# The end of each stage token tile by token tile: the last two output blocks finish the first tile early, and the second tile is normalised in halves on two engines

## The reference

```
f = swiglu(rms_norm(x, g0)) ;  x = x + 0.5 * rms_norm(f, g1)      # ffn0 -> "p0"
m = short_conv_mixer(rms_norm(x, g2)) ;  x = x + rms_norm(m, g3)  # conv -> "pc"
f = swiglu(rms_norm(x, g4)) ;  x = x + 0.5 * rms_norm(f, g5)      # ffn1 -> "p1"
k, v = rms_norm(x, g_kv) @ w_kv
...                                                               # ffn2 -> "p2", attention -> "pa", ffn3 -> "p3"
swiglu(h) = (silu(h @ w_gate) * (h @ w_up)) @ w_down              # 1024 -> 2816 -> 1024
```

## Time and profile before

| | |
|---|---|
| median of 3 runs | 2194.36 us (2194.2 to 2194.81) |
| the profiled execution's own time | 2194.22 us |
| its span in the profile | 2192.4 us |
| busy: PE / DVE / ACT / POOL | 88% / 59% / 35% / 19% |
| chain that ended last | PE 65%, DMA 15%, DVE 8%, POOL 4%, ACT 3% |
| mean granted TensorE clock | 0.927 |

### The profile page before, as it was taken

The page is one execution under the profiler, slowest core; times in us unless marked ns, Lnnn a source line. Parts: engine busy times, 40 slices in busy tenths (PEclk is TensorE's granted clock), DMA queues, the critical chain, the costliest instruction groups (busy, mean ns, idle before and its releaser), DMA issues.

```text
span 2192.4 us, 30637 instructions
## 1 busy us (share of the span) xinstructions
PE 1919.4 (88%) x11270; PEld 1548.3 (71%) x11270; DVE 1285.4 (59%) x2435; ACT 765.1 (35%) x1183; POOL 416.8 (19%) x536
## 2 busy tenths in 40 slices
PE   7988889968877778788779998989989999868998
PEld 7977789963333333333249998989989999758997
DVE  4443475588777777777564446654454444565444
ACT  4343414331212222212123444344444433454342
POOL 3000000045555545545410001000010000110000
PEclk9986899989989988989989999999999999969999
DMA  8312316549999999999965554545545555404552
GB/s 220 106 51 77 77 58 164 173 186 421 421 422 422 422 421 421 422 423 421 423 226 180 190 188 149 177 158 191 184 152 172 192 177 187 134 29 155 181 191 96
DMA packets 231409, 496.65 MB, mean 227 GB/s; under 512 B 21653, under 2 KB 182566, under 8 KB 198566
## 3 DMA queue, kind: packets, MB, share of 16 engines
q1 hardware_dynamic: 188432, 221.36, 32.1%
q0 software_dynamic: 38224, 273.04, 30.2%
q10 hardware_dynamic: 4678, 1.21, 0.3%
HBM read 494.53 MB, written 1.05 MB: 226 GB/s over the span
## 4 chain that ended last, share of the span: by engine, by line
PE 65%; DMA 15%; DVE 8%; POOL 4%; issue 4%; ACT 3%; DVEq 0%; POOLq 0%; ACTq 0%
PE ps L1733 42%; PE acc L1733 22%; DMA rows_hi<-in_peer_uv,idx_now 13%; DMA rows_xh<-in_peer_uv,idx_now 2%; POOL raw L614 1%; POOL arena L614 1%; PE acc L1790 1%; POOL rstd L532 1%; ACT hi L669 1%; DVE arena L1460 1%; DVE arena L1456 1%; DVE lo L1107 1%; DVE arena L1463 1%; DVE arena L1682 0%; POOL idx_now L609 0%
## 5 line engine op out<-in xcount | busy, mean ns | idle before, releaser
L1107 DVE TENSOR_TENSOR lo<-raw,hi 128x2048 fp32r<-128x2048 f32 x210 | 479.2, 2283 | 397.5 <-ACT hi L669 397.4
L1733 PE MATMUL ps<-xh,hi 128*128 128x256 f32 x2184 | 626.9, 287 | 14.1 <-DVE xl L1128 8.4
L1733 PE MATMUL ps<-xl,hi 128*128 128x256 f32 x2184 | 622.9, 285 | 0.0
L1733 PE MATMUL ps<-xh,lo 128*128 128x256 f32 x2184 | 622.5, 285 | 0.0
L669 ACT ACTIVATE hi<-raw 128x2048 fp32r<-128x2048 f32 x210 | 400.0, 1905 | 334.9 <-PE ps L1733 277.6
L1733 PEld LDWEIGHTS ps<-xh,hi 128*128 128x128 f32 x2184 | 423.6, 194 | 20.5 <-issue 13.1
L1733 PEld LDWEIGHTS ps<-xl,hi 128*128 128x128 f32 x2184 | 423.8, 194 | 1.5
L1733 PEld LDWEIGHTS ps<-xh,lo 128*128 128x128 f32 x2184 | 423.3, 194 | 0.1
L529 POOL TENSOR_SCALAR ss<-ss 128x1 f32<-128x1 f32 (+2 forms) x34 | 11.6, 341 | 1179.8 <-ACT arena L996 938.6
L1733 PE MATMUL acc<-arena,diag 128*128 128x512 f32 x384 | 188.0, 638 | 51.0 <-ACT diag L942 50.7
L1733 PE MATMUL acc<-rows,diag 128*128 128x512 f32 x192 | 117.6, 777 | 85.7 <-ACT diag L942 75.5
(11 more groups left out here) (274 smaller groups left out, 2848.8 us busy)
## 6 DMA issues: line engine op xcount, KB each, us to landing
raw<-in_w_ffn_gate SPq DMA_DIRECT2D x44, 1024.0 KB, 5.3
raw<-in_w_ffn_up SPq DMA_DIRECT2D x44, 1024.0 KB, 5.3
...
```

Of the source, the lines that this page charges most:

```text
L1107: v.tensor_tensor(lo[s][:, 0:WORDS[p]], raw[s][:, 0:WORDS[p]], hi[s][:, 0:WORDS[p]].bitcast(F32), ALU.subtract).then_inc(lo_done, 1)
L1733: return nc.tensor.matmul(out, l, r, start=first, stop=last)
```

## The change

In the **ffns**, PE's last two down panels change order: down(9) and down(10) of the first tile, then `branch_half`, then down(9) and down(10) of the second (`down_part`). In the **projections** the last two panels do the same. ACT and DVE split only the first of the next two panels before `post`. The second one's high part (`SECOND`) is written by ACT inside `post`, and its low part by POOL, in a new 128x2048 `tensor_tensor` after POOL's norms; DVE waits for it before its next split.

In **`post`** the first tile's squares for the next norm move from ACT to DVE. The second tile goes in halves of 512 columns (`HALVES`): ACT squares each half of `ACC`, DVE multiplies by the gain and updates x half by half, ACT squares the first half of x and DVE the second, POOL adds the two sums (its `tensor_scalar` takes the second sum as an operand; the scale moves into the squares), and DVE writes the first half of the rows, ACT the second (`rows_half`, for which PE waits ahead of the third pair of transposes). `SUMS`, `X_AT` and `PRODUCTS` are the counts that go with this.

```diff
@@ -145,10 +145,21 @@
...
+HALVES = 2
+TWO = [n for pair in POSTS for n in pair if n]
+SUMS = [SUMS, {n: sum(0 if m in HEAD_NORMS else HALVES if m in TWO else 1 for m, *_ in NORMS[:k + 1]) for k, (n, *_) in enumerate(NORMS)}]
...
+STEPS = 1 + HALVES
...
+SECOND = {"p0": FIRST["conv_in"] + 1, "pc": FIRST["ffn1"] + 1, "p1": FIRST["kv"] + 1, "p2": FIRST["q"] + 1, "pa": FIRST["ffn3"] + 1}
...
@@ -525,8 +537,11 @@
                 _, w, scale, factor = NORMS[k]
                 c = slice(t * w // TT, (t + 1) * w // TT)
                 m, rs = ss[:, k, c], rstd[:, k, c]
-                pool.wait_ge(*{"hg": (hg_sq, TT * HG_HEADS), "diff": (df_sq, TT * DIFF_HEADS)}.get(name, (sumsq[t], SUMS[name])))
-                g.tensor_scalar(m, m, scale / factor ** 2, EPS / factor ** 2, ALU.mult, ALU.add).then_inc(rstd_step, 1)
+                pool.wait_ge(*{"hg": (hg_sq, TT * HG_HEADS), "diff": (df_sq, TT * DIFF_HEADS)}.get(name, (sumsq[t], SUMS[t][name])))
+                if t and name in TWO:
+                    g.tensor_scalar(m, m, ss[:, k, 2:3], BIAS[name], ALU.add, ALU.add).then_inc(rstd_step, 1)
+                else:
+                    g.tensor_scalar(m, m, 1.0 if name in TWO else SCALE[name], BIAS[name], ALU.mult, ALU.add).then_inc(rstd_step, 1)
                 rstd_steps[0] += 1
                 pool.wait_ge(rstd_step, rstd_steps[0])
                 g.tensor_tensor(rs, m, minus_half[:, c], ALU.pow).then_inc(rstd_ready[t], 1)
...
@@ -623,8 +638,17 @@
             def post(name):
                 load_gain(name)
                 norm(name)
+                if name not in SECOND:
+                    return
+                norm(dict(POSTS)[name])
+                p = SECOND[name]
+                pool.wait_ge(lo_done, p)
+                pool.wait_ge(hi_done, p + 1)
+                b = p % SLOTS
+                g.tensor_tensor(lo[b][:, :], raw[b][:, :], hi[b][:, :].bitcast(F32), ALU.subtract).then_inc(lo_done, 1)
...
@@ -982,27 +1001,33 @@
                 split(p0 + 5, 3, i - 1)
                 silu(p0 + 2, 3, i - 1)
                 upper(p0 + 2, p0, 3, i - 1, fh)
-                for p in range(last + 1, min(last + 3, NP)):
-                    split(p)
+                if last + 1 < NP:
+                    split(last + 1)
             def post(name, panels):
                 k, after = NIDX[name], dict(POSTS)[name]
-                for t in range(TT):
-                    act.wait_ge(*((branch_half, [n for n, _ in POSTS].index(name) + 1) if t == 0 else (panel_used, panels)))
-                    act.wait_ge(sumsq[1 - t], SUMS[name] - 1 + t)
-                    nc.scalar.activation(sq_dump, ACC[:, 2 * t:2 * t + 2, :].rearrange("p b n -> p (b n)"), ACT.Square,
-                                         accum_out=ss[:, k, t:t + 1]).then_inc(sumsq[t], 1)
+                act.wait_ge(branch_half, POST_AT[name] + 1)
+                act.wait_ge(sumsq[1], SUMS[1][name] - HALVES)
+                nc.scalar.activation(sq_dump, ACC[:, 0:2, :].rearrange("p b n -> p (b n)"), ACT.Square, scale=SCALE[name] ** 0.5,
+                                     accum_out=ss[:, k, 0:1]).then_inc(sumsq[0], 1)
+                if name in SECOND:
+                    split(SECOND[name])
+                act.wait_ge(panel_used, panels)
+                act.wait_ge(sumsq[0], SUMS[0][name])
+                for b in range(HALVES):
+                    nc.scalar.activation(sq_dump[:, b * 512:(b + 1) * 512], ACC[:, 2 + b, :], ACT.Square, scale=SCALE[name] ** 0.5,
+                                         accum_out=ss[:, k, 1 + b:2 + b]).then_inc(sumsq[1], 1)
                 if after is None:
                     return
                 k = NIDX[after]
-                act.wait_ge(x_updated, X_AT[name] - 1)
-                act.wait_ge(sumsq[1], SUMS[after] - 1)
-                nc.scalar.activation(sq_dump, x[:, 0, :], ACT.Square, accum_out=ss[:, k, 0:1]).then_inc(sumsq[0], 1)
                 act.wait_ge(rstd_ready[0], k + 1)
                 nc.scalar.activation(xn[:, 0, :], x[:, 0, :], ACT.Copy, scale=rstd[:, k, 0:1]).then_inc(rows_ready[0], 1)
+                act.wait_ge(x_updated, X_AT[name] - 1)
+                act.wait_ge(sumsq[1], SUMS[1][name])
+                nc.scalar.activation(sq_dump[:, 0:512], x[:, 1, 0:512], ACT.Square, scale=SCALE[after] ** 0.5, accum_out=ss[:, k, 1:2]).then_inc(sumsq[1], 1)
+                act.wait_ge(rstd_ready[1], k + 1)
+                nc.scalar.activation(xn[:, 1, 512:], x[:, 1, 512:], ACT.Copy, scale=rstd[:, k, 1:2]).then_inc(rows_half, 1)
                 turn(after, xh, after)
...
@@ -1579,30 +1604,44 @@
                 split(p0 + 5, 3, i - 1)
                 product(p0 + 3, i, 3, i - 1)
                 rest(i, fh, fl)
-                for p in range(last + 1, min(last + 3, NP)):
-                    split(p)
+                if last + 1 < NP:
+                    split(last + 1)
             def post(name):
                 k, after = NIDX[name], dict(POSTS)[name]
-                u = TT * (1 + [n for n, _ in POSTS].index(name))
+                u, n = PRODUCTS[name] - STEPS, X_AT[name] - STEPS
                 dve.wait_ge(spread_loaded, 16 * (SPREAD.index(name) + 1))
                 dve.wait_ge(turned, XBASE[after] if after else XEND["f3"])
-                for t in range(TT):
-                    dve.wait_ge(sumsq[t], SUMS[name])
-                    v.tensor_tensor(xn[:, t, :], ACC[:, 2 * t:2 * t + 2, :].rearrange("p b n -> p (b n)"), gb[:, :], ALU.mult).then_inc(gain_used, 1)
-                    dve.wait_ge(gain_used, u + t + 1)
-                    dve.wait_ge(rstd_ready[t], k + 1)
-                    v.scalar_tensor_tensor(out=x[:, t, :], in0=xn[:, t, :], scalar=rstd[:, k, t:t + 1], in1=x[:, t, :],
+                dve.wait_ge(sumsq[0], SUMS[0][name])
+                v.tensor_tensor(xn[:, 0, :], ACC[:, 0:2, :].rearrange("p b n -> p (b n)"), gb[:, :], ALU.mult).then_inc(gain_used, 1)
+                dve.wait_ge(gain_used, u + 1)
+                dve.wait_ge(rstd_ready[0], k + 1)
+                v.scalar_tensor_tensor(out=x[:, 0, :], in0=xn[:, 0, :], scalar=rstd[:, k, 0:1], in1=x[:, 0, :],
+                                       op0=ALU.mult, op1=ALU.add).then_inc(x_updated, 1)
+                if after:
+                    dve.wait_ge(x_updated, n + 1)
+                    v.scalar_tensor_tensor(out=xn[:, 0, :], in0=x[:, 0, :], scalar=SCALE[after], in1=x[:, 0, :], op0=ALU.mult, op1=ALU.mult,
+                                           accum_out=ss[:, NIDX[after], 0:1]).then_inc(sumsq[0], 1)
+                half = [slice(b * 512, (b + 1) * 512) for b in range(HALVES)]
+                for b in range(HALVES):
+                    dve.wait_ge(sumsq[1], SUMS[1][name] - HALVES + 1 + b)
+                    v.tensor_tensor(xn[:, 1, half[b]], ACC[:, 2 + b, :], gb[:, half[b]], ALU.mult).then_inc(gain_used, 1)
+                dve.wait_ge(gain_used, u + STEPS)
+                dve.wait_ge(rstd_ready[1], k + 1)
+                for b in range(HALVES):
+                    v.scalar_tensor_tensor(out=x[:, 1, half[b]], in0=xn[:, 1, half[b]], scalar=rstd[:, k, 1:2], in1=x[:, 1, half[b]],
                                            op0=ALU.mult, op1=ALU.add).then_inc(x_updated, 1)
                 if after is None:
                     return
                 k = NIDX[after]
                 dve.wait_ge(x_updated, X_AT[name])
-                square(x[:, 1, :], xn[:, 1, :], ss[:, k, 1:2]).then_inc(sumsq[1], 1)
+                v.scalar_tensor_tensor(out=xn[:, 1, half[1]], in0=x[:, 1, half[1]], scalar=SCALE[after], in1=x[:, 1, half[1]], op0=ALU.mult, op1=ALU.mult,
+                                       accum_out=ss[:, k, 2:3]).then_inc(sumsq[1], 1)
                 dve.wait_ge(rstd_ready[1], k + 1)
-                v.tensor_scalar(xn[:, 1, :], x[:, 1, :], rstd[:, k, 1:2], None, ALU.mult).then_inc(rows_ready[1], 1)
+                v.tensor_scalar(xn[:, 1, half[0]], x[:, 1, half[0]], rstd[:, k, 1:2], None, ALU.mult).then_inc(rows_ready[1], 1)
                 turn(after, xh, xl, after)
+                dve.wait_ge(lo_done, SECOND[name] + 1)
...
@@ -1785,6 +1824,8 @@
                 for t in range(TT):
                     pe.wait_ge(rows_ready[t], XIDX[name] + 1)
                     for b in range(XEND[name] - XBASE[name]):
+                        if t and b == 2 and name in TWO:
+                            pe.wait_ge(rows_half, [after for _, after in POSTS].index(name) + 1)
                         for j in range(2):
                             c = (2 * b + j) * P
...
@@ -2056,20 +2097,22 @@
-                def down(p, i, m=0, r=0, first=False, final=False):
+                def down_part(p, t, halves=range(2), u=(ah, al), first=False, final=False):
+                    wh, wl = views(p, 2)
+                    for half in halves:
+                        for k in range(2):
+                            c, w = slice(t * P, (t + 1) * P), slice(half * 512, (half + 1) * 512)
```

(23 more changed lines are left out.)

72 lines of the change are left out of this document (33 added, 39 removed).

## The result

The change takes 2216.62 us (median of 4 runs, 2208.41 to 2217.43) against 2194.28 for the kernel before (4 runs, 2192.69 to 2194.81): a ratio of 1.0123, with a 95% interval of 1.0084 to 1.0162, so 22 us slower. The forecast was 2188.2, with a range up to 2193.2.

The account below looks back on a forecast made before the run. PE, busy 88%, was taken to bound the kernel, idling at stage ends: three ffn ends save 1.75 us each, two projection ends 0.45, the last 0; together 6.1 off 2194.22 gives 2188.2 us, range 2185.8 to 2193.2.

Parts of the forecast that it names:

- the first rival: At five stage ends POOL's subtraction starts first and DVE's half rows wait for all of it: about 2211 us; 9%.
- the pair at 8.57: Earlier-trace race behind one power: DVE first by 0.05, its 0.75 stood, POOL's 0.19 became 0.75; cited against POOL winning.
- 1 us either way: Behind stage ends, PE's granted clock may recover later: 1 us either way in the sum, not a case of its own.
- Before E: E starts ACT's squares of the second tile; PE's reorder costs nothing, tile 0's squares end E-0.4, ACT's high part E-0.8.
- From E to the update: Second tile's halves after E: power ends E+2.25, update E+3.75 against E+3.77 before, so halves bring nothing here.
- The sixth end: The end behind ffn3, where only the output store follows the update of x: gain 0.
- The rstd of tile 0: POOL's next-norm steps for the first tile: rstd there at E+3.5, first transposes at E+4.83.
- The third rival: Tile 0's rstd comes one half of DVE's update later: first product E+9.6, 2191.5 us; 19%.
- The gap: E to the next stage's first product: 8.9 us at five ends, against 10.67 at three ffn and 9.35 at two projection ends.
- POOL's subtraction: The second panel's low part on POOL: 4.6 us, E+6.8 to E+11.4, hidden by 3.3 us before PE wants it.
- the second rival: POOL's subtraction holds DVE's low part `xl` for 3.1 us at five ends: 2203 us; 4%.

Follow-up runs that it names:

- experiment 1: The change, with POOL's subtraction also waiting until DVE has written its half of the rows: ratio 0.9978.
- experiment 2: The change with no subtraction on POOL; DVE does it behind its `xl` parts: ratio 1.0002.
- experiment 5: The change plus one small POOL instruction between the power and the subtraction, tried in two forms; first form timed: 2183.46 us, ratio 0.9975.
- experiment 7: The change with POOL's norm steps in tile order: subtraction waiting for DVE's half rows, ratio 0.9997; subtraction on DVE instead, 0.998.
- experiment 4: The kernel before with only the subtraction moved to POOL, made to wait for DVE's last row of the next norm: ratio 0.9974.
- experiment 3: The kernel before with one part of the change each: POOL's unordered subtraction alone, ratio 1.0096; PE's new order of products alone, 1.0076.

## Why the prediction was wrong

**The step that failed** is the weighing of the first rival, "POOL takes DVE's way": the prediction let DVE's half of the rows start ahead of the subtraction, at 0.5 us, and it started 0.07 behind and took 4.71. The rival's mechanism, its place and its price were right: a half row that waits for the whole subtraction, at five ends, 17 us, 2211; measured +22. I gave it 9%. What I put against it was that the subtraction waits on two satisfied semaphores, and that the POOL step with one such wait came second in the pair at 8.57. In the change these waits cost nothing. POOL had worked off the first of them before the power began: in the chain above its record, POOLq L649, stands at 1329.66, the power at 1329.70. The subtraction then started 0.03 to 0.04 ahead of the power's end, like the memset of the earlier trace rows, which was first by 0.08. The step L544 of the change, also behind a power and with a wait, started 0.09 behind the power's end (1326.51 and 1326.60), as its counterpart in the earlier trace rows did. The two races of the earlier trace rows thus spoke for both sides, and I went by the one with the wait. With one pair for each side and 50 ns between them, even chances were the most that these rows bore, and a forecast near 2188 with a range up to 2193 was not to be drawn from them.

The trace of before held more than these two. At four of the five stage ends POOL's next load of the gain stands right behind this very power, and its one semaphore has been satisfied since DVE's last gain ended (1326.34 at ffn0). At ffn0's end, POOL and then DVE:

```profile
1329.68 0.55 POOL L532 TENSOR_TENSOR rstd<-ss,minus_half 128x1 f32<-128x1 f32 x1
1330.18 0.95 POOL L594 DMA_DIRECT2D gb<-in_g_norm  x1
...
1330.26 0.75 DVE L1604 TENSOR_SCALAR xn<-x,rstd 128x1024 f32<-128x1024 f32 x1 [1.34 <-POOL rstd L532]
```

It starts 0.05 ahead of the power's end and 0.08 ahead of DVE's rows, with a satisfied wait, and 0.08 or 0.09 ahead of them at the other three. It does not hold DVE up, whose rows keep their 0.75, but it shows who comes first in the place where the change puts the subtraction. With the memset and the norm step of the earlier trace rows, which was ahead by 0.02 (1954.04 and 1954.06), these are six starts of POOL ahead of DVE, against the one behind at 8.57.

**What the rival's sum left out**: the clock. Its gaps came out as priced, 16.2 us longer; the other 6.5 are the products behind them at a lower granted clock. I had put "1 us either way" for it, from one product of 0.55 instead of 0.28. The windows show 4.8 us in the first 20 us of the five stages and 1.7 in the low spell of the first. Of the same kind is the miss in experiments 1, 2, 5 and 7: had the order been right, I would have forecast 6.1 us and got between -0.1 and 2.8.

**Before E: right.** DVE's squares of tile 0 end at E-0.38 (1322.58 + 1.23 - 1324.19), forecast E-0.4, and ACT's high part at E-0.74 (1321.53 + 1.92), forecast E-0.8. PE's new order cost nothing by itself: the stage lengths of the kernel with that order alone are within 0.5 of those before at the four later stages. Its first stage is 2.4 longer (97.40 and 95.02), but with the old order experiment 4 has 96.87 there, at the same low spell. That it needs DVE's split out of the way was in the step, "DVE does one split less", and experiment 3 shows what it is worth: 14.5 us of gaps.

**From E to the update: right but for ffn0.** The power ends at E+2.32 (1326.51 - 1324.19), forecast E+2.25. The update ends at E+3.84 at four ends, forecast E+3.75, and at ffn0 at E+4.22, since DVE started it there 0.48 behind the power and not 0.12; why is open. The sixth end gains nothing: last E to the end of the span is 8.44, before 8.15, so it even loses 0.3.

**The rstd of tile 0: right within 0.3.** Forecast E+3.5, measured E+3.23 at ffn0, where POOL's power began 0.12 ahead of DVE's update and ran its 0.55 (1326.87 and 1326.99), and E+3.6 at the other four ends (1437.05 + 0.92 - 1434.38), where the update was first and the power took 0.92, as forecast. The first transposes start at E+4.55 and E+4.9, forecast E+4.83. The third rival (one half later) did not occur, but that is luck as much as reckoning: at those four ends POOL's step began 0.02 ahead of the update (E+2.40 and E+2.42).

**The gap: right where the race is out of it.** E+8.9 was forecast at all five ends; in experiments 1, 2 and 5 it is 8.9 once and 9.2 four times. The sum of gaps is 45.8, forecast 44.5; four times 0.3 is the difference.

**POOL's subtraction: right.** 4.50 us, forecast 4.6; the Trainium skill's figure ("GPSIMD Engine Reference", "Elementwise — side-by-side cycle accounting") is 4497 ns, which the trace bears out. It is hidden when it starts behind the rows. It never held `xl`, the second rival: with the subtraction running from E+6.8 to E+11.3 at ffn0 in experiment 1, DVE's four `xl` of 1.66 us ran as they do in the change, where POOL had nothing (both 1.66).

```profile
1331.04 1.66 DVE L1154 SCALAR_TENSOR_TENSOR xl<-acc,cols,xh 128x256 fp32r<-128x256 f32 x4 [1.65 <-ACT xh L728]
```

**The rule that I quoted and did not act on.** The half row and the subtraction start 0.07 us apart in the change and 0.15 apart in experiment 5. Whoever was first kept its own length while the other lasted until the first had ended and longer: 4713 ns for the half row and 4496 for the subtraction in the change, 487 and 4763 in experiment 5. The Trainium skill's "SBUF — State Buffer", section "Who interferes with whom", says so in advance: the engine that issues first keeps the shared ports until its instruction ends. The trace agrees. By that rule a long instruction on one of the two engines is a risk of its own length for the other, whoever looks likelier to be first.
